# Attention block of a streaming encoder step: the stick leads, and cached memory keys are multiplied by masked queries that accumulate in place

## The chip, the cores and the metric

The kernel runs on one core of one Trainium2 chip. The metric is the device time of one execution in microseconds; of several runs the median is taken. Everything is float32.

## The reference, cut to what matters

One layer of an encoder is computed for a prompt of 1024 frames and for a batch of 8 samples of 16 frames each, which share the weights. The 8 x 16 sample frames are put together into one tile of 128 rows. After a combined projection there are three kinds of attention:

```
A (the "stick"): z = q.k/8; log_keep = -softplus(z) under a strict causal mask;
   weight = exp(log_sigmoid(z) + sum of log_keep of the later keys); out = weight @ v      8 heads of 64
B (the "window"): softmax over 128 past keys and the own chunk, with ALiBi and sinks       8 q heads, 2 kv heads of 64
M (the "memory"): softmax over 256 memory tokens, no mask                                  4 heads of 128
```

Every one of the 8 samples has its own caches: 128 past keys and values for A, 128 for B, 256 for M. A query of sample b may meet the cached keys of sample b alone. After the attention come the gated output projection and a retrieval of single experts (128 per frame) from a table of 16384, which takes most of the time and is not touched.

## The kernel before, in words

`build` (1600s) calls three blocks in turn, `project`, `attend` and `experts`. A block is a program per engine; the next one begins when all engines have come to its end.

`attend` works on tiles of 128 queries: 8 of the prompt (t = 0 to 7) and the sample tile (t = 8, called ST). Its order is written by the class `Course`. It deals out everything to ticks `tau`, and every engine walks through the ticks in order, doing at each whatever the course lists for it. Engines aren't tied to one tick together: only semaphores hold them.

- **Stick.** A step is one tile of queries against one tile of keys; each step occupies two ticks, each tile one more. Step k has its products with the keys at its first tick (`score`, PE, L756), then the chain Abs, Exp, Ln on ScalarE (L809 to L813), the softplus and its mask on VectorE (L837, L843), the sum over later keys as a product with a triangle (`suffix`, PE, L624 and L627), the weights (L770, or L852, L775 and L868 for the first step of a tile), and six ticks after the score the product with the values (L687). The order of tiles is 0, ST, 1, 2, ... 7, the first step at tick 4. The second step of ST is against the cached keys: 8 samples by 8 heads of small products, 64 rows by 128 keys, 16 queries each, from the tile `cache`, which `cache_kT` fills; later `cache` takes the cached values.
- **Window and memory.** 27 units (t, c), three per tile, ST first: c = 0 and 1 are halves of the window's heads, c = 2 is the memory attention. A unit makes its logits (`wscore`, PE, L642 to L650), adds a bias and takes the maximum on VectorE (L882, L888), exponentiates on ScalarE (L789), normalises (L910), is transposed on PE (L699) and copied (L797), and multiplied with the values. The units stand every three ticks from tick 7 on, and seven ticks after unit 2. The logits of all of them lie in PSUM banks 4 and 5.
- **Cached keys of window and memory** (`mul`, ticks 1 to 4, L653 to L667). For each sample b, 8 products for the memory (`kmem[b]`, 128 keys as the stationary operand, 16 query columns moving; L661) and 2 for the window (`kwcT`, 64 columns; L666). The results have keys in rows, so ScalarE copies them out of PSUM (`past_m` L800, `past_w` L801) and the units of ST transpose them back with the identity (L644, L650). `kmem` has three buffers, which SyncE refills as `mul_done` counts. The cached values of the memory go through the same buffers at ticks 19 to 22 (`past_values`, L738).

SyncE issues the loads in this order: bias, sinks, `kwcT`, `vwc`, `kmem` for samples 0 to 2, `cache_kT`. PSUM banks 0 to 3 hold the stick's logits, 4 and 5 the units' logits, 6 the transposes and outputs of the units, 7 the output of the stick. GpSimd does nothing in this block.

The heart of the old arrangement, in code:

```
for kk in range(2):
    for h in range(MH):
        nc.tensor.matmul(ps[:, 4 + kk, h * P + b * DS:h * P + (b + 1) * DS],
                         kmem[:, b % 3, h * MT + kk * P:h * MT + (kk + 1) * P], qm[:, h, c], start=True, stop=True)
```

Of the kernel before, what the change touches and what calls it, by code (L numbers as in the profile page):

```python
# [24 lines left out]
P = 128  # L25
# [3 lines left out]
ST = PT  # L29
# [408 lines left out]
class Course:  # L438


    def __init__(self):
        self.steps = []
        b = 4
        self.order = [0, ST] + list(range(1, ST))
# [17 lines left out]
        self.mul_at = 1  # L462
        self.win = []
        b = self.mul_at + 6
        for u in range(len(self.units)):
            self.win.append(b)
            b += 7 if u == 2 else 3
# [28 lines left out]
def attend(nc, A, S, wide_dram, o_d):  # L496
# [7 lines left out]
    with ExitStack() as ctx:  # L504
# [8 lines left out]
        vcache = cache[:, :].rearrange("p (b n) -> p b n", b=DB)  # L513
        bias = sb("bias", [P, SWH, 2 * P])
# [4 lines left out]
        past_m = sb("past_m", [P, 2, MH, P])  # L519
# [24 lines left out]
        kw_in = sem("kw_in")  # L544
        km_in = [sem(f"km_in{i}") for i in range(3)]
        mul_done = sem("mul_done")
        past_kept = sem("past_kept")
# [19 lines left out]
        def _(sp):  # L567
# [8 lines left out]

            sp.dma_start(bias[:, :, :].rearrange("p h k -> p (h k)"), wide_dram[:, BW:2 * BW]).then_inc(bias_in, 16)
            sp.dma_start(sink[:, :], A["sinks"][0:1, :].to_broadcast([P, SWH])).then_inc(sink_in, 16)
            sp.dma_start(kwcT[:, :, :].rearrange("p b s -> p (b s)"), A["cache_swa_kT"]).then_inc(kw_in, 16)
            sp.dma_start(vwc[:, :, :], A["cache_swa_v"][0].rearrange("b s h d -> s b (h d)")).then_inc(kw_in, 16)  # L580
            for n in range(3):
                load_mem(n)
            sp.dma_start(kcache, A["cache_kT"]).then_inc(kc_in, 16)
            for tau in range(C.length):
# [9 lines left out]
                if tau in C.mul:  # L594
                    k = C.mul[tau]
                    for b in range(2 * k, 2 * k + 2):
                        sp.wait_ge(mul_done, b + 1)
                        load_mem(b + 3)
                if tau in C.wfront and C.wfront[tau] == 2:
# [15 lines left out]

        @block.tensor
        def _(pe):
            for tau in range(C.length):
# [10 lines left out]
                if tau in C.wscore:  # L629
# [4 lines left out]
                    if t == ST and c == 0:  # L634
                        pe.wait_ge(past_kept, 2)
                    out = ps[:, 4:6, :].rearrange("p a (j k) -> p (a j) k", k=2 * P)
                    cols = slice(t * P, (t + 1) * P)
                    for i in (0, 2, 1, 3):
# [7 lines left out]
                        elif t < ST:  # L646
                            last = nc.tensor.matmul(out[:, i, :], qm[:, i, cols], mk[:, i, :], start=True, stop=True)
                        else:
                            for kk in range(2):
                                last = nc.tensor.transpose(out[:, i, kk * P:(kk + 1) * P], past_m[:, kk, i, :], ident)  # L650
                    last.then_inc(w_logits, 1)
                if tau in C.mul:
                    m = C.mul[tau]  # L653
                    if m == 0:
                        pe.wait_ge(kw_in, 32)
# [1038 lines left out]
```

## Time and profile before

| | us |
|---|---|
| median of 3 runs | 4359.3 (4357.4 to 4360.08) |
| the profiled execution, its own time | 4359.77 |
| span of that execution | 4357.9 |
| of it the block of attention, 429.6 to 903.3 us | 473.7 |
| TensorE busy, share of the span | 82% |
| VectorE / ScalarE / GpSimd busy | 60% / 34% / 40% |

The span is the stretch that the profile covers; the execution's own time is 1.9 us longer. Busy times of TensorE (PE) are sums over its matrix products, whose ends are modelled; PEld is the loading of stationary operands. PEclk in a row is the clock granted to TensorE as a share of its full speed: 0.50 is 1.2 GHz, 1.00 is 2.4 GHz. One float32 product of the program stands as two PE instructions in the trace, a transpose as one.

### The profile page before, as it was taken

To read this page: it belongs to the slowest core of one execution; us is meant where nothing else is said; L and a number is where in the kernel's file an instruction comes from. 1 tells how busy PE (TensorE), PEld (TensorE's weight loads), DVE (VectorE), ACT (ScalarE), POOL (GpSimd) and SP (SyncE) were. 2 spreads that over 40 slices of the span, in tenths; PEclk is the share of its full clock that TensorE was granted. 3 is DMA by queue.
4 is the path that set the end of the run, shared out by engine and by line. 5 is a ranking of instruction groups with operands and counts; after the bars stand their busy time and mean duration, and the time that the engine had idled before them with its cause. 6 is when DMAs were issued, how large, how long until landed. Compare 5 with 4: busy or idle time off the path is not lost.

```text
span 4357.9 us, 35532 instructions
## 1 busy us (share of the span) xinstructions
PE 3565.2 (82%) x11041; PEld 1831.4 (42%) x11041; DVE 2595.4 (60%) x5556; ACT 1491.4 (34%) x3932; POOL 1744.5 (40%) x1430
## 2 busy tenths in 40 slices
PE   7999888889668898858888888996777777778777
PEld 4545655568434445423333345442333333333222
DVE  2130256621778954866876876676676676676444
ACT  2111256721343334343333335344222222223222
POOL 0000000000456677666676666667333333333332
PEclk9999589999879999979998998998999999999999
DMA  5111310044889899999999999999999999999998
GB/s 168 56 38 59 113 42 20 16 145 167 335 330 387 350 420 422 407 385 421 421 421 421 411 419 421 421 397 417 421 421 421 419 420 417 414 416 412 422 421 355
DMA packets 246270, 1415.48 MB, mean 325 GB/s; under 512 B 26417, under 2 KB 58417, under 8 KB 92721
## 3 DMA queue, kind: packets, MB, share of 16 engines
q0 software_dynamic: 165888, 1208.03, 67.4%
q1 hardware_dynamic: 80192, 205.18, 12.7%
q8 instruction: 87, 1.43, 0.1%
q14 instruction: 103, 0.84, 0.1%
HBM read 1374.85 MB, written 39.19 MB: 324 GB/s over the span
## 4 chain that ended last, share of the span: by engine, by line
DMA 24%; POOL 17%; PE 15%; DVE 11%; issue 10%; ACT 3%; POOLq 0%; SPq 0%; ACTq 0%; DVEq 0%
DMA ring<-in_experts_dram,idx 24%; POOL side L1232 9%; PE ps L1342 8%; POOL ring L1221 7%; DVE ring L1596 4%; PE ps L1313 2%; PE ps L1265 2%; PE ps L1290 1%; ACT diag L1440 1%; DVE cand L1471 1%; PE ps L1275 1%; DVE hot L1486 1%; DVE hot L1482 1%; DVE idx L1490 1%; DVE part L1479 1%
## 5 line engine op out<-in xcount | busy, mean ns | idle before, releaser
L1342 PE MATMUL ps<-ring,diag 128*128 128x512 f32 x3520 | 1794.6, 655 | 655.7 <-ACT diag L1440 642.1
L1221 POOL DMA_INDIRECT ring<-in_experts_dram,idx x1152 | 1101.4, 956 | 2528.4 <-PE ps L1342 1281.0
L1596 DVE CUSTOM_DVE_ANT_0 ring<-ring,ps 128x1024 f32<-128x1024 f32 x1152 | 1385.8, 1220 | 877.7 <-DMA ring<-in_experts_dram,idx 864.5
L1342 PEld LDWEIGHTS ps<-ring,diag 128*128 128x128 f32 x3520 | 696.6, 206 | 1659.1 <-ACT diag L1440 909.8
L1424 ACT ACTIVATE act_<-hid 128x2 f32<-128x2 f32 x576 | 117.1, 203 | 2021.7 <-DVE hid L1596 2016.2
L1232 POOL TENSOR_TENSOR side<-side,ring 128x1024 f32<-128x1024 f32 x272 | 642.6, 2362 | 56.2 <-ACT ring L1445 50.7
L1265 PE MATMUL ps<-hx,wbuf 128*128 128x256 f32 (+2 forms) x1152 | 402.9, 494 | 13.6 <-DMA hx<-hT_scratch 13.0
L1440 ACT ACTIVATE diag<-const,wgt 128x128 f32<-128x128 f32 x880 | 320.5, 396 | 19.5 <-PE ps L1342 0.7
L1445 ACT ACTIVATE ring<-ring,wgt 128x1024 f32<-128x1024 f32 x272 | 308.1, 1133 | 0.0
L1265 PEld LDWEIGHTS ps<-hx,wbuf 128*128 128x128 f32 x1152 | 224.6, 195 | 184.0 <-issue 118.1
L309 PE MATMUL ps<-w_qkv,hT 128*128 128x512 f32 (+1 forms) x720 | 285.1, 552 | 1.3 <-DVE mhT L403 1.3
L1431 ACT ACTIVATE wgt<-act_,gw 128x1 f32<-128x1 f32 x1152 | 276.8, 287 | 19.8
L1313 PE MATMUL ps<-hx,wbuf 128*128 128x256 f32 (+2 forms) x768 | 269.8, 500 | 13.8 <-ACT mixn L1393 12.6
L837 DVE SCALAR_TENSOR_TENSOR sps<-ps,za 128x512 f32<-128x512 f32 x76 | 52.4, 690 | 277.3 <-ACT za L813 277.3
L1313 PEld LDWEIGHTS ps<-hx,wbuf 128*128 128x128 f32 x768 | 152.3, 199 | 131.8 <-issue 98.1
L1275 PE MATMUL ps<-o_x,wbuf 128*128 128x256 f32 (+2 forms) x576 | 203.5, 490 | 0.0
L309 PEld LDWEIGHTS ps<-w_qkv,hT 128*128 128x128 f32 x720 | 134.8, 191 | 132.0 <-issue 126.4
L412 DVE TENSOR_REDUCE nrm<-stage 128x4 f32<-128x512 f32 (+2 forms) x29 | 16.3, 562 | 239.4 <-ACT stage L355 239.4
L1275 PEld LDWEIGHTS ps<-o_x,wbuf 128*128 128x128 f32 x576 | 111.3, 193 | 84.2 <-issue 58.5
L1290 PE MATMUL ps<-wbuf,mixn 128*128 128x256 f32 x576 | 129.8, 382 | 1.6 <-DVE mixn L1540 1.6
L1290 PEld LDWEIGHTS ps<-wbuf,mixn 128*128 128x128 f32 x576 | 110.7, 192 | 29.3 <-issue 15.4
L624 PE MATMUL ps<-sps,const 128*128 128x512 f32 x152 | 93.6, 701 | 25.6 <-DVE sps L843 19.6
(174 smaller groups left out, 2782.8 us busy)
## 6 DMA issues: line engine op xcount, KB each, us to landing
wbuf<-in_w_gate_o_dram SPq DMA_DIRECT2D x72, 768.0 KB
wbuf<-in_w_q_dram SPq DMA_DIRECT2D x24, 1024.0 KB
ring<-in_experts_dram,idx POOLq DMA_INDIRECT x1152
wbuf<-in_w_out_dram SPq DMA_DIRECT2D x12, 1024.0 KB
w_qkv<-in_w_in_dram SPq DMA_DIRECT2D x5, 2048.0 KB, 8.2
o_x<-o_scratch SPq DMA_DIRECT2D x9, 768.0 KB, 26.6
s<-s_scratch SPq DMA_DIRECT2D x6, 1024.0 KB, 11.1
hT_scratch<-hT SPq DMA_DIRECT2D x9, 512.0 KB, 6.7
```

Of the source, the lines that this page charges most:

```text
L309: last = nc.tensor.matmul(ps[:, bank(u), 0:n], src[:, k, t * P:(t + 1) * P], w[:, c % 2, k, 0:n], start=(k == 0), stop=(k == KC - 1))
L1221: i = nc.gpsimd.indirect_dma_start(out=ring[:, j % RING, :], out_offset=None, in_=A["experts"], in_offset=bass.IndirectOffsetOnAxis(ap=idx ...
L1232: nc.gpsimd.tensor_tensor(side[:, m % 2], side[:, m % 2], ring[:, j % RING, DM:2 * DM], ALU.add).then_inc(side_done, 1)
L1265: last = nc.tensor.matmul(ps[:, 4 + u % 2, 0:N].rearrange("p (i t) -> p i t", t=P), w[:, k * P:(k + 1) * P], hx[:, 0:n, k, :], start=(k == ...
L1275: last = nc.tensor.matmul(ps[:, 6 + u % 2, 0:N].rearrange("p (i t) -> p i t", t=P), w[:, k * P:(k + 1) * P], o[:, 0:n, b, k - KC, :], star ...
L1290: last = nc.tensor.matmul(ps[:, 4 + x % 4, 0:2 * P], mixn[:, k * N + i * P:k * N + (i + 1) * P], w[:, k * 2 * P:(k + 1) * 2 * P], start=(k ...
L1313: last = nc.tensor.matmul(ps[:, 4 + x % 2, 0:N].rearrange("p (i t) -> p i t", t=P), w[:, c:c + P], hx[:, 0:n, k, :], start=(k == 0), stop= ...
L1342: last = nc.tensor.matmul(acc[:, h, :], diag[:, (by_pe(j) - 1) % 4, :], ring[:, j % RING, DM + h * HB:DM + (h + 1) * HB], start=(j % SLOTS ...
L1431: last = nc.scalar.activation(wgt[:, i:i + 1], act_[:, i:i + 1], ACT.Copy, scale=gw[:, m % 2, i:i + 1])
L1440: last = nc.scalar.activation(diag[:, d % 4, :], ident, ACT.Copy, scale=wgt[:, j % SLOTS:j % SLOTS + 1])
L1445: nc.scalar.activation(v, v, ACT.Copy, scale=wgt[:, j % SLOTS:j % SLOTS + 1]).then_inc(scaled, 1)
L1596: last = nc.vector.tensor_tensor_reduce(out=u, in0=u, in1=xp, scale=1.0, scalar=0.0, op0=ALU.mult, op1=ALU.add, accum_out=hid[:, j % SLOTS ...
```

## The change

- The stick begins at tick 0 and not 4, and the order of tiles is 0, 1, 2, 3, ST, 4 to 7. Its steps on ST are at ticks 24 and 26.
- The window's products with `kwcT` all go to tick 2, into PSUM banks 5 and 6; a single copy (`past_w`) follows. `kwcT` is the first load.
- The units of ST begin at ticks 4, 7 and 13; those of the prompt stay at ticks 20, 23, ... 89. The course is 97 ticks long as before.
- The products with the cached memory keys go to ticks 10 to 13, two samples each. GpSimd clears the tile `cache` and writes into it, for each sample and head, the queries of the sample tile with zeros in place of all other samples' queries (`qz`). That is the stationary operand now, 256 keys move, and the 8 samples accumulate on one another in PSUM banks 4 and 5. What stands there in the end are the logits of unit 2 with queries in rows: `past_m`, its copy and its transposes are gone.
- The stick's first values no longer wait for the two copies, and the window's values of unit 0 wait for `vwc` by a semaphore of its own.
- `cache_kT` is loaded into `cache` only when these products are done (SyncE, tick 14).

```diff
@@ class Course
-        b = 4
-        self.order = [0, ST] + list(range(1, ST))
+        b = 0
+        self.order = [0, 1, 2, 3, ST] + list(range(4, ST))
@@
-        self.mul_at = 1
-        self.win = []
-        b = self.mul_at + 6
-        for u in range(len(self.units)):
+        self.swa_at = 2
+        self.mul_at = 10
+        self.win = [4, 7, self.mul_at + 3]
+        b = self.win[2] + 7
+        for u in range(3, len(self.units)):
             self.win.append(b)
-            b += 7 if u == 2 else 3
+            b += 3
@@ attend
+        qz = cache[:, :].rearrange("p (h b q) -> p h b q", h=MH, b=DB)
-        past_m = sb("past_m", [P, 2, MH, P])
@@ sync
+            sp.dma_start(kwcT[:, :, :].rearrange("p b s -> p (b s)"), A["cache_swa_kT"]).then_inc(kw_in, 16)
             sp.dma_start(bias[:, :, :].rearrange("p h k -> p (h k)"), wide_dram[:, BW:2 * BW]).then_inc(bias_in, 16)
             sp.dma_start(sink[:, :], A["sinks"][0:1, :].to_broadcast([P, SWH])).then_inc(sink_in, 16)
-            sp.dma_start(kwcT[:, :, :].rearrange("p b s -> p (b s)"), A["cache_swa_kT"]).then_inc(kw_in, 16)
-            sp.dma_start(vwc[:, :, :], A["cache_swa_v"][0].rearrange("b s h d -> s b (h d)")).then_inc(kw_in, 16)
+            sp.dma_start(vwc[:, :, :], A["cache_swa_v"][0].rearrange("b s h d -> s b (h d)")).then_inc(vw_in, 16)
             for n in range(3):
                 load_mem(n)
-            sp.dma_start(kcache, A["cache_kT"]).then_inc(kc_in, 16)
@@
                     for b in range(2 * k, 2 * k + 2):
-                        sp.wait_ge(mul_done, b + 1)
+                        if b < DB - 1:
+                            sp.wait_ge(mul_done, b + 1)
+                        else:
+                            sp.wait_ge(w_logits, 3)
                         load_mem(b + 3)
+                if tau == C.mul_at + 4:
+                    sp.wait_ge(w_logits, 3)
+                    sp.dma_start(kcache, A["cache_kT"]).then_inc(kc_in, 16)
@@ new: GpSimd
+        @block.gpsimd
+        def _(pool):
+            nc.gpsimd.memset(cache[:, :], 0.0).then_inc(zeroed, 1)
+            pool.wait_ge(zeroed, 1)
+            for b in range(DB):
+                c = slice(b * DS, (b + 1) * DS)
+                last = nc.gpsimd.tensor_copy(qz[:, :, b, c], qm[:, :, ST * P + b * DS:ST * P + (b + 1) * DS])
+            last.then_inc(qz_done, 1)
@@ tensor
-                if tau in C.wscore:
+                if tau in C.wscore and C.wscore[tau] != 2:
@@
-                        pe.wait_ge(past_kept, 2)
+                        pe.wait_ge(past_kept, 1)
@@
+                if tau == C.swa_at:
+                    pe.wait_ge(kw_in, 16)
+                    for b in range(DB):
+                        c = slice(ST * P + b * DS, ST * P + (b + 1) * DS)
+                        for gg in range(KVH):
+                            r = slice(gg * HD, (gg + 1) * HD)
+                            out = ps[:, 5 + gg, :].rearrange("p (j q) -> p j q", j=GRP)[:, :, b * DS:(b + 1) * DS]
+                            last = nc.tensor.matmul(out, kwcT[r, b, :], qw[r, :, c], start=True, stop=True)
+                    last.then_inc(swa_done, 1)
                 if tau in C.mul:
                     m = C.mul[tau]
                     if m == 0:
-                        pe.wait_ge(kw_in, 32)
+                        pe.wait_ge(qz_done, 1)
+                        pe.wait_ge(w_exped, 2)
                     for b in range(2 * m, 2 * m + 2):
-                        c = slice(ST * P + b * DS, ST * P + (b + 1) * DS)
                         pe.wait_ge(km_in[b % 3], 16 * (b // 3 + 1))
...
-+                        for h in range(MH):
+                            last = nc.tensor.matmul(ps[:, 4 + h // 2, (h % 2) * MT:(h % 2 + 1) * MT], qz[:, h, b, :], kmem[:, b % 3, h * MT:(h + 1) * MT],
+                                                    start=(b == 0 and h % 2 == 0), stop=(b == DB - 1), skip_group_check=True)
+                        last.then_inc(mul_done if b < DB - 1 else w_logits, 1)
...
@@ scalar
-                if tau == C.mul_at + 4:
-                    act.wait_ge(mul_done, DB)
-                    nc.scalar.activation(past_m[:, :, :, :].rearrange("p k h q -> p (k h q)"), ps[:, 4:6, :].rearrange("p a n -> p (a n)"), ACT.Copy).then_inc(past_kept, 1)
-                    nc.scalar.activation(past_w[:, :, :].rearrange("p h q -> p (h q)"), ps[:, 6:8, :].rearrange("p a n -> p (a n)"), ACT.Copy).then_inc(past_kept, 1)
+                if tau == C.swa_at:
+                    act.wait_ge(swa_done, 1)
+                    nc.scalar.activation(past_w[:, :, :].rearrange("p h q -> p (h q)"), ps[:, 5:7, :].rearrange("p a n -> p (a n)"), ACT.Copy).then_inc(past_kept, 1)
```

## Rows read from the trace of the kernel before

**Rows 1.** The page: its span and the busy time of each engine

```profile
span 4357.9 us, 35532 instructions
...
PE 3565.2 (82%) x11041; PEld 1831.4 (42%) x11041; DVE 2595.4 (60%) x5556; ACT 1491.4 (34%) x3932; POOL 1744.5 (40%) x1430
```

**Rows 2.** Stretches of attention: length, busy time by engine, TensorE clock, DMA share, GB/s

```profile
429.60:473.90 44.30, 32.89 (x160) 31.79 (x160) 0.00 (x0) 1.28 (x1) 0.00 (x0) 0.52 0.61 214
473.90:518.70 44.80, 36.30 (x212) 26.39 (x210) 17.38 (x29) 16.47 (x32) 0.00 (x0) 0.50 0.17 59
518.70:554.00 35.30, 27.94 (x342) 19.54 (x340) 16.82 (x30) 20.89 (x47) 0.00 (x0) 0.94 0.16 46
554.00:592.60 38.60, 38.59 (x234) 28.20 (x234) 17.87 (x29) 13.20 (x29) 0.00 (x0) 0.78 0.32 89
592.60:876.50 283.90, 244.94 (x1805) 153.97 (x1804) 174.10 (x299) 198.28 (x456) 0.00 (x0) 0.98 0.06 17
876.50:903.30 26.80, 20.86 (x157) 14.65 (x156) 12.96 (x22) 12.45 (x32) 0.00 (x0) 0.94 0.11 30
```

**Rows 3.** Timeline, 441 to 474 us: start, duration, engine, operation, idle time before it

```profile
441.01 3.57 PE L661 MATMUL ps<-qmT,kmem 128*128 128x16 f32 x16 [12.21 <-DMA kmem<-in_cache_mem_kT_dram]
...
444.51 0.69 PE L666 MATMUL ps<-qswT,kwcT 64*128 64x64 f32 x4
...
473.92 1.83 PEld L756 LDWEIGHTS ps<-qsbT,ksbT 64*128 64x128 f32 x16
```

**Rows 4.** Transfer of the window's cached keys, issue to landing

```profile
DMA to landing us min/median/max: 7.4/7.4/7.4
```

**Rows 5.** Timeline of the stick's start, 474 to 492 us

```profile
474.02 2.02 PE L756 MATMUL ps<-qsbT,ksbT 64*128 64x128 f32 x16
...
477.92 1.01 ACT L800 ACTIVATE past_m<-ps 128x1024 f32<-128x1024 f32 x1
...
479.51 2.07 PE L624 MATMUL ps<-sps,const 128*128 128x512 f32 x2 [3.47 <-DVE sps L843]
...
483.15 2.08 PE L624 MATMUL ps<-sps,const 128*128 128x512 f32 x2 [1.56 <-DVE sps L843]
...
489.13 2.12 PE L756 MATMUL ps<-qsbT,ksbT 64*128 64x128 f32 x15
```

**Rows 6.** Timeline: cached keys and values of the stick, and a product at the clock's rise

```profile
499.73 10.83 PE L756 MATMUL ps<-qsbT,cache 64*128 64x16 f32 x100
...
518.71 1.66 PE L624 MATMUL ps<-sps,const 128*128 128x512 f32 x2
...
537.88 3.91 PE L687 MATMUL ps<-wts,cache 128*64 128x16 f32 x128
```

**Rows 7.** Timeline: cached memory values (128x16), memory logits of a prompt tile (128x256)

```profile
565.94 3.74 PE L738 MATMUL ps<-PTs,kmem 128*128 128x16 f32 x32
...
887.19 1.89 PE L647 MATMUL ps<-mkT,qmT 128*128 128x256 f32 x8
```

**Rows 8.** Waits from 592.6 to 876.5 us: us in total, times, longest

```profile
DVE sps L837 <- ACT za L813: 96.6, 44, 4.6
...
ACT za L809 <- PE ps L756: 31.0, 21, 3.9
```

**Rows 9.** GpSimd's instructions, grouped by line

```profile
L1232 POOL TENSOR_TENSOR side<-side,ring 128x1024 f32<-128x1024 f32 x272 | 642.6, 2362 | 56.2 <-ACT ring L1445 50.7
...
L260 POOL MEMSET kswT<- 128x128 f32 x1 | 0.2, 206 | 0.3 <-POOLq L1659 0.3
```

**Rows 10.** Short stretches about an idle time of TensorE, columns as in group 2

```profile
530.00:533.00 3.00, 0.99 (x2) 0.16 (x2) 2.93 (x5) 0.17 (x1) 0.00 (x0) 1.00 0.00 0
533.00:536.00 3.00, 2.24 (x14) 1.94 (x16) 2.24 (x5) 0.60 (x1) 0.00 (x0) 0.58 0.00 0
536.00:540.00 4.00, 4.00 (x83) 3.02 (x82) 0.93 (x2) 3.03 (x7) 0.00 (x0) 0.89 0.02 4
```

**Rows 11.** Timeline: the first product of the next block

```profile
915.49 5.53 PE L1265 MATMUL ps<-hx,wbuf 128*128 128x256 f32 x16 [13.00 <-DMA hx<-hT_scratch]
```

More of the change, by code:

```diff
@@ L544, in attend @@
         kw_in = sem("kw_in")
+        vw_in = sem("vw_in")
         km_in = [sem(f"km_in{i}") for i in range(3)]
         mul_done = sem("mul_done")
+        swa_done = sem("swa_done")
+        zeroed = sem("zeroed")
+        qz_done = sem("qz_done")
         past_kept = sem("past_kept")
@@ L645, in _ @@
                             last = nc.tensor.matmul(out[:, i, P:2 * P], qw[r, j, cols], kw[r, NT * P:(NT + 1) * P], start=True, stop=True)
-                        elif t < ST:
+                        else:
                             last = nc.tensor.matmul(out[:, i, :], qm[:, i, cols], mk[:, i, :], start=True, stop=True)
-                        else:
-                            for kk in range(2):
-                                last = nc.tensor.transpose(out[:, i, kk * P:(kk + 1) * P], past_m[:, kk, i, :], ident)
                     last.then_inc(w_logits, 1)
+                if tau == C.swa_at:
[7 more added lines that the diff above has]
+                    last.then_inc(swa_done, 1)
                 if tau in C.mul:
@@ L654, in _ @@
                     if m == 0:
-                        pe.wait_ge(kw_in, 32)
+                        pe.wait_ge(qz_done, 1)
+                        pe.wait_ge(w_exped, 2)
                     for b in range(2 * m, 2 * m + 2):
-                        c = slice(ST * P + b * DS, ST * P + (b + 1) * DS)
                         pe.wait_ge(km_in[b % 3], 16 * (b // 3 + 1))
-                        for kk in range(2):
-                            for h in range(MH):
-                                nc.tensor.matmul(ps[:, 4 + kk, h * P + b * DS:h * P + (b + 1) * DS],
-                                                 kmem[:, b % 3, h * MT + kk * P:h * MT + (kk + 1) * P], qm[:, h, c], start=True, stop=True)
-                        for gg in range(KVH):
-                            r = slice(gg * HD, (gg + 1) * HD)
-                            out = ps[:, 6 + gg, :].rearrange("p (j q) -> p j q", j=GRP)[:, :, b * DS:(b + 1) * DS]
-                            last = nc.tensor.matmul(out, kwcT[r, b, :], qw[r, :, c], start=True, stop=True)
-                        last.then_inc(mul_done, 1)
+                        for h in range(MH):
+                            last = nc.tensor.matmul(ps[:, 4 + h // 2, (h % 2) * MT:(h % 2 + 1) * MT], qz[:, h, b, :], kmem[:, b % 3, h * MT:(h + 1) * MT],
+                                                    start=(b == 0 and h % 2 == 0), stop=(b == DB - 1), skip_group_check=True)
+                        last.then_inc(mul_done if b < DB - 1 else w_logits, 1)
                 if tau in C.values:
@@ L674, in _ @@
                             pe.wait_ge(st_kept, C.nth(t))
-                        else:
-                            pe.wait_ge(past_kept, 2)
                     else:
@@ L704, in _ @@
                     pe.wait_ge(pt_kept, 2 * u + 2)
+                    if u == 0:
+                        pe.wait_ge(vw_in, 16)
                     probs = lambda i, kk: PTs[:, (2 * i + kk) * P:(2 * i + kk + 1) * P]
```

## The prediction

> **What bounds the kernel now.** I read the page first: TensorE is busy for 82% of the span, more than any other engine, but that is a mean over three blocks [rows 1]. The change lies in attention alone, so the table by stretches comes next [rows 2]. Attention runs from 429.6 to 903.3 us, and the next block cannot start before all engines have left it: its first product is at 915.49 us after 13.00 us without PE work, which end with a transfer that is issued only then [rows 11]. So what attention gains or loses at its end shifts all that follows by the same amount, and I forecast that end.
>
> The stretches show three regimes. From 429.6 to 473.9 us nothing but the cached-key products runs: VectorE does nothing, ScalarE one table load, and PE waits for `kmem` at first (12.21 us, part of which lies before the block) [rows 2, 3]. In the timeline the stick's first product comes right behind, at 473.92 us. The clock is 0.50 throughout. From 473.9 to 518.7 us it is still 0.50, and from then on mostly full. In the steady stretch from 592.6 to 876.5 us PE is busy for 244.94 of 283.90 us and ScalarE for 198.28; the waits there are VectorE on ScalarE's chain and that chain on the stick's logits [rows 8]. PE is thus close to the bound, and its order within a tick feeds the chain.
>
> As a yardstick, that stretch goes from the score of tick 24 to that of tick 86, 62 ticks: 4.58 us a tick. Ticks 11 to 18 took 35.30 us, 4.41 a tick. The clock matters for narrow products as well: 16 of them (128x16) took 3.57 us at 0.50, 32 took 3.74 us near 1.00, so 0.223 against 0.117 us each [rows 3, 7]. Had they run at full clock, the 128 old memory products would have taken 15 us and not 28.6.
>
> **The change part by part, as a timetable of attention.** The removed front is 473.9 - 430.0 = 43.9 us: after it the stick's first product starts at 430.0.
>
> *Ticks 0 to 3.* The old start, score at 474.02, suffixes at 479.51 and 483.15, next score ending at 491.25, took 17.2 us at 0.50; it held 3.9 us of unit 0's logits between 485.2 and 489.1 [rows 5]. The new one has no logits of a unit there, but the 16 window products of `kwcT`. Four of their instructions take 0.69 us at 0.50 [rows 3], about 0.62 net of overlap, so 8 samples take 5.0 us. The copy of `past_m` (1.01 us, which stood ahead of the chain's second half) is gone, that of `past_w` is behind both halves. The first suffix can start at 5.5 us, so PE is then busy without a gap: 435.5 + 2.1 + 5.0 + 2.1 + 2.1 = 447. `kwcT` landed 7.4 us after its issue with a megabyte ahead of it [rows 4]; it is now first, so at 437 at the latest, when PE wants it at 437.6. Its new wait has the second suffix and score 1 queued behind it and through them the whole chain; I cost it at nothing (0 to 2 us).
>
> *Ticks 4 to 9.* These are 6 ticks of ordinary work: 26.4 us at 4.41. At half clock PE's own work is the bound: logits of units 0 and 1 (2 x 3.9), suffixes (2.1 three times, 4 twice with `later`), two scores, two values, two transposes: 31 us. I take 28, with the clock rising within. Tick 10 starts at 475.
>
> *Ticks 10 to 13.* To each, two samples are added: 8 samples by 4 heads are 32 products, 64 instructions with 256 columns moving. Eight such took 1.89 us at full clock, 1.73 net of the last one's overlap [rows 7]: 64 are 14 us. At 0.50 they would be 28. They stand ahead of the score, so they delay the chain and are not hidden beside it; only PE's idle share (14%, some 2 us) takes a part. Four ticks are 18.3 + 14 - 2 = 30, and tick 14 starts at 505. The clock is what separates 14 from 28. The rows of the steady stretch show 0.98 with PE idle 14% of the time, and one loss: after 3 us with 0.99 busy the next stretch had 0.58 and the one after 0.89 [rows 2, 10]. These new products are wide and leave no gaps, so I take the full clock. The Trainium skill speaks against it: in "TensorE: Matmul & The Clock Gate", section "Loop structure matters more than you think", products that stand between waits run at the low clock; by it this term is 28 us and attention ends 14 us later (the rival of half clock below).
>
> *What they wait for.* `qz_done`: GpSimd clears 4096 elements a row and makes 8 copies of 64. By its clearing of 128 elements in 206 ns that is at most 6.6 us, by its two-input addition (1024 in 2362 ns) 9.4 us [rows 9]; the copies add 1 to 2. It ends by 442, 33 us early; cover gone only if GpSimd is five times slower. `kmem` for samples 0 to 2 arrives as before, at 441 or sooner. Later samples have over 7 us a tick to come. SyncE now waits for the stick's output of tile 1 ahead of the load for sample 7: 0 to 2 us, taken as 0. `cache_kT`, once `cache` is free at tick 14, has 12 ticks until it is wanted. The eight transposes of `past_m` (1 us) vanish.
>
> *Ticks 14 to 18.* 5 x 4.41 = 22: to 527. *Ticks 19 to 23* have the same work as before, cached memory values included, which with its clock of 0.78 took 38.6 us [rows 2]: to 566.
>
> *Ticks 24 to 81.* 58 x 4.58 = 265.6. In them now lie the stick's cached keys, 128 narrow instructions. They took 13.8 us at 0.50 (100 in 10.83 us [rows 6]); scaled as above they are 7.3 at full clock. Less the ordinary score, that adds 6 to 12.6; they leave PE's array mostly idle, and the clock may fall behind them, so I take 10. The cached values took 3.91 against 1.1 us: 2.8 more. That leads to 844. In the Trainium skill, same page, section "LDWEIGHTS (loading the stationary operand)", a load of 128 columns takes 107 ns at either clock; by that the keys always cost 13.7 us and the end comes some 2.6 us later. Rows 3 and 7 show that the load-bound product follows the clock.
>
> *Tick 82 to the end.* The stick's last score was at tick 86 and is at tick 82, while the units stay at their ticks. Before, 26.8 us were left after it [rows 2]. Now four more ticks lie between it and the last unit. With one unit at a time each engine waits for the other, about 7 us for three ticks (logits 1.5, VectorE 3, ScalarE 2.5), so 9 us more; at least 5, at most 4 x 4.58 = 18. 844 + 26.8 + 9 = 880.
>
> **Sum.** Attention ends at 880 and not at 903.3: 23 us earlier. Against the profiled execution's span of 4357.9 this is 4335, with 1.9 us around it 4337. That execution's own time, 4359.77, lies 0.5 above the median of the runs shown, so the median comes to 4336. A difference of 0.2%, 9 us, is about what a measurement of this kernel can tell from none.
>
> **The rivals.**
>
> *Half clock in ticks 4 to 13.* The chain's start leaves PE with gaps, as between 474 and 496. For it: 0.50 until 518.7 before. Against it: those gaps came from work that was too little per tick, and the rise at 518.7 (two wide products in 1.66 us where 2.07 was the price [rows 5, 6]) came after 8 us of dense ordinary products, which the new ticks 2 to 7 offer too. It costs 14 us at the cached keys and 5 in the ticks: attention ends near 899, time 4355, no change. Chance 0.10.
>
> *The gain is larger.* The end is less ragged and the cached keys go by at full clock (-6 together), the new products fill the slack of the chain (-4): 4325. What speaks for it: 96.6 us of waits of VectorE for the chain [rows 8]. Chance 0.15.
>
> *Slower.* The clock stays low from the start through the stick's cached keys at tick 26. A steady tick has 3.95 us of PE work at full clock, near 7 at half, so each loses about 2.3 us. It needs 14 us at the memory keys and 8 more ticks at half clock to eat the 23 us; if 22 such ticks in 4 to 31 are slow, the loss is 14 + 50 - 23: 4400. Before, ticks 11 to 18 had 0.94 under the same load, which speaks against it. Chance 0.03.
>
> *It doesn't do what it says.* A late tile, `kwcT` or a `kmem` buffer, takes the place of the old wait: 12 us at most, as before, and the end is at 892, time 4348. Chance 0.09.
>
> **How the numbers follow.** The forecast has a chance of 0.63, within 4330 to 4345 for its terms (start 0 to 4, tail -4 to +9, cached keys -4 to +3). With the larger gain below and the late tile above, the range is 4322 to 4350; half clock and slower lie outside. Faster by over 0.2% is under 4350.6: 0.63 + 0.15 + 0.09, and a little of half clock, 0.88. Within 0.2%: 0.09. Slower: 0.03.
>
> **What the changed profile would show.** Right: the first stick product at 430, nothing idle at the block's head; the window products ahead of the second suffix; 64 instructions 128x256 on `kmem` in all 14 us at a clock near 1.00; the attention's end near 880; a last unit after the stick with PE half idle. Wrong: 0.50 in the row of ticks 10 to 13, PE's wait on `kwcT`, `kmem` or GpSimd, more than 13 us at the stick's cached keys, or over 40 us from the last stick score to the end. If the end moves and the whole does not by the same amount, the claim that attention's end gates the next block is false.

## The result and the profile after

The changed kernel takes 4312.94 us (median of 5 executions, 4311.97 to 4328.63) beside 4357.54 for the kernel before (5 executions), a ratio of 0.9911 with a 95% interval of 0.99 to 0.9921. I had forecast 4336, 4322 to 4350: the direction was right and the gain nearly twice as large, outside the range. Two more series, of the same code, gave 4318.19 and 4327.40. The 15 executions of all three have a median of 4319.1; they lie between 4312.0 and 4319.1 or between 4326.1 and 4330.9, with none between.

The page of the profiled execution, which took 4311.97 us:

```profile
span 4310.2 us, 35396 instructions
...
PE 3524.2 (82%) x10969; PEld 1800.8 (42%) x10969; DVE 2591.9 (60%) x5556; ACT 1490.8 (35%) x3931; POOL 1746.8 (41%) x1439
```

Stretches of attention, cut at the ticks that the prediction used (PE begins a tick with its suffix, and 24 and 82 are cut at their score, as in the prediction): 0 to 3, 4 to 9, 10 to 13, 14 to 18, 19 to 23, 24 to 81, and the rest; columns as in [rows 2].

```profile
427.10:441.60 14.50, 10.87 (x69) 7.36 (x69) 4.20 (x6) 6.42 (x9) 5.45 (x9) 0.67 0.72 255
441.60:464.30 22.70, 18.61 (x108) 10.96 (x108) 17.39 (x30) 15.80 (x36) 0.00 (x0) 0.91 0.05 13
464.30:491.10 26.80, 26.79 (x212) 20.61 (x212) 11.10 (x19) 13.57 (x26) 0.00 (x0) 1.00 0.50 146
491.10:509.60 18.50, 14.84 (x105) 8.91 (x101) 7.34 (x12) 9.48 (x21) 0.00 (x0) 0.82 0.52 201
509.60:542.00 32.40, 32.40 (x238) 24.21 (x238) 16.36 (x27) 15.34 (x32) 0.00 (x0) 1.00 0.37 106
542.00:816.30 274.30, 240.79 (x1893) 158.02 (x1892) 164.14 (x281) 183.71 (x422) 0.00 (x0) 0.95 0.08 25
816.30:856.40 40.10, 28.36 (x213) 20.11 (x212) 18.60 (x32) 17.75 (x52) 0.00 (x0) 0.91 0.07 20
```

Attention now goes from 427.1 to 856.4 us, 429.3 in place of 473.7, 44.4 less. The project block before it happened to end 2.5 us earlier. What follows did not change: from its first product to the end of the span are 3441.6 us, and were 3442.4 [rows 1, 11]. So the claim that the end of attention gates the rest holds. The most telling columns are PE busy and PEclk: PE's work in ticks 19 to 23 has become shorter at the same count of ordinary steps, with the clock at 1.00 where [rows 2] had 0.78. Added up over stretches of 4 us, weighed by their clock, TensorE stood at 0.50 for some 126 us of attention before and 55 now. Of these 55, some 14 lie at the stick's cached keys and right behind them (551 to 571 us). Some 21 more begin at two idle times of PE: 14 at the start of the block, behind 3.56 us, and 7 at tick 17, behind 3.66 us; both stand in the timeline that follows.

Steps of the timetable in the timeline of the changed kernel, PE alone:

```profile
427.17 1.16 PE L776 MATMUL ps<-qsbT,ksbT 64*128 64x128 f32 x16 [0.83 <-PEq L87]
...
431.89 2.07 PE L643 MATMUL ps<-sps,const 128*128 128x512 f32 x2 [3.56 <-DVE sps L862]
433.90 3.68 PE L675 MATMUL ps<-qswT,kwcT 64*128 64x64 f32 x32
...
437.50 2.07 PE L643 MATMUL ps<-sps,const 128*128 128x512 f32 x2
...
465.28 3.66 PE L685 MATMUL ps<-kmem,cache 128*128 128x256 f32 x16
...
501.83 2.07 PE L643 MATMUL ps<-sps,const 128*128 128x512 f32 x2 [3.66 <-DVE sps L862]
...
552.02 11.34 PE L776 MATMUL ps<-qsbT,cache 64*128 64x16 f32 x128
...
563.28 2.07 PE L643 MATMUL ps<-sps,const 128*128 128x512 f32 x2
...
868.61 3.77 PE L1284 MATMUL ps<-hx,wbuf 128*128 128x256 f32 x8 [13.01 <-DMA hx<-hT_scratch]
```

A pair of suffix instructions (L643) is a good gauge of the clock: it takes about 1.1 us at 1.00 and 2.07 at 0.50. The first score starts at once, the window's products stand ahead of the second suffix, and the masked products of two samples (16 instructions) take 3.66 us at full clock. The stick's cached keys take 11.34 us at tick 26, begun at full and ended at half clock, and the suffix behind them still costs 2.07 us.

GpSimd's part, grouped by line:

```profile
L628 POOL MEMSET cache<- 128x4096 f32 x1 | 3.5, 3516 | 426.0 <-POOLq L87 426.0
L632 POOL COPY cache<-qmT 128x64 f32<-128x64 f32 x8 | 1.9, 290 | 0.1
```

### The profile page after: what moved, and what is told of

Same layout as the page of the kernel before. It is cut to its first block, busy times and chain, and to the rows that moved or that the text cites. A ratio compares the mean times of both kernels' runs of the same rounds, so it can differ in the third digit from the quotient of the medians.

```text
span 4310.2 us, 35396 instructions
## 1 busy us (share of the span) xinstructions
PE 3524.2 (82%) x10969; PEld 1800.8 (42%) x10969; DVE 2591.9 (60%) x5556; ACT 1490.8 (35%) x3931; POOL 1746.8 (41%) x1439
## 4 chain that ended last, share of the span: by engine, by line
DMA 24%; POOL 17%; PE 15%; DVE 12%; issue 10%; ACT 3%; POOLq 0%; SPq 0%; ACTq 0%; DVEq 0%
DMA ring<-in_experts_dram,idx 23%; POOL side L1251 10%; PE ps L1361 8%; POOL ring L1240 8%; DVE ring L1615 4%; PE ps L1332 2%; PE ps L1284 2%; PE ps L1309 1%; PE ps L1294 1%; ACT diag L1459 1%; DVE cand L1490 1%; DVE hot L1505 1%; DVE hot L1501 1%; DVE part L1498 1%; DVE idx L1509 1%
```

## The experiments

Times are medians in us, with the ratio to the kernel before, run in the same series, and its 95% interval. The experiments ran in four series, and the kernel before had 4359.6 to 4361.5 us in them; where two runs of different series are compared, the ratios are the fairer measure. "Attention" is read from the one profiled execution, from the block's first instruction to the copy of the last unit's output.

| kernel | time | ratio | attention |
|---|---|---|---|
| before | 4357.5 to 4361.5 | 1 | 473.6 |
| stick first alone | 4358.5 | 0.9997 (0.9988 to 1.0007) | 471.0 |
| stick first, sample tile late | 4349.5 | 0.9981 (0.9971 to 0.9991) | 467.0 |
| the same, masked wide products at ticks 1 to 4 | 4331.2 | 0.9935 (0.9919 to 0.9952) | 449.8 |
| changed kernel, three series | 4312.9, 4318.2, 4327.4 | 0.9911, 0.9906, 0.9922 | 429.2, 430.2, 440.0 |
| changed, narrow products at ticks 10 to 13 | 4338.8 | 0.9945 (0.9927 to 0.9964) | 457.1 |
| the same, 128 columns each | 4320.9 | 0.9907 (0.9893 to 0.992) | 442.8 |
| before, masked products alone | 4347.0 | 0.9967 (0.9958 to 0.9977) | 464.7 |
| masked products and stick first, old order | 4358.9 | 1.0002 (0.9993 to 1.0011) | 474.6 |
| changed, masked stick keys | 4322.7 | 0.9915 (0.9902 to 0.9929) | 435.8 |
| changed, values split | 4314.6 | 0.9898 (0.9882 to 0.9915) | 429.9 |
| both of these | 4313.7 | 0.9902 (0.9887 to 0.9918) | 429.2 |

**Stick first alone.** The old course with one number changed:

```diff
-        b = 4
+        b = 0
```

> The kernel before with the stick's steps beginning at tick 0 and nothing else changed: cached memory keys in the old narrow form at ticks 1 to 4, tile ST second. The first score runs at once, but the second score stands behind samples 0 to 5 of the cached keys, which still wait for the transfer (441 us) and run at 1.20 GHz (4.15 us a sample). Theory 'clock': narrow products keep the clock low whatever stands between them, so only the start-up of the first step (about 15 us of idle PE between 474 and 489) is hidden: 10 to 16 us faster, 4342 to 4348. Rival 'order': most of the 44 us comes from the stick leading, so 25 us or more faster, under 4333.

Neither theory had it: no gain. PE in its timeline:

```profile
429.47 1.16 PE L756 MATMUL ps<-qsbT,ksbT 64*128 64x128 f32 x16 [0.83 <-PEq L87]
...
440.83 3.57 PE L661 MATMUL ps<-qmT,kmem 128*128 128x16 f32 x16 [10.20 <-DMA kmem<-in_cache_mem_kT_dram]
...
468.96 2.02 PE L756 MATMUL ps<-qsbT,ksbT 64*128 64x128 f32 x16
```

The first score runs at 429.47, but PE works in order, the second stands behind six samples, and these wait for the transfer as before; it comes at 468.96. That is 5 us earlier than the old first score at 474.0. The units of the window now end further behind the stick: 41.1 us from its last score to the end, 26.8 before [rows 2], and of the cached keys' cost nothing is saved, 13.84 us at half clock.

**The order of tiles in addition.**

```diff
-        self.order = [0, ST] + list(range(1, ST))
+        self.order = [0, 1, 2, 3, ST] + list(range(4, ST))
```

> The run in which the stick's steps begin at tick 0 and all else is old, with the new order of tiles in addition (0, 1, 2, 3, sample, 4 to 7). The stick's cached keys then no longer follow directly on the narrow products of ticks 1 to 4. Theory 'clock': between the two narrow blocks the clock has risen, so the cached keys take 11 and not 13.9 us, and the ticks behind the front are ordinary and fast: 5 to 12 us faster than the run with the old order, 4347 to 4354. Rival 'order is nothing': within 3 us of it, 4356 to 4361.

9 us faster than the run before it (7 by the ratios, as the series differ), within the range of theory "clock". Its cached keys took 8.8 us where they had taken 13.8.

**The masks in addition, still at ticks 1 to 4** (the products as in the change; their result is copied once, and unit 2 reads the copy).

> Stick from tick 0, new order of tiles, masked wide products, but these still at ticks 1 to 4, where PE waits for the first transfer until 439 us with the stick's second score behind. The run with the old order of tiles lost its gain to a wait for the stick's keys (8 us) and the narrow keys at half clock behind it; both are gone here. Theory 'clock': masked against narrow products is worth 10 to 16 us beside the run with the late sample tile alone, and what is still missing to the changed kernel is the waiting at the front (10 us) and a little more: 4326 to 4336. Rival 'place is nothing': equal to the changed kernel, 4313 to 4320.

18 us faster again in the same series, a little more than the 10 to 16 that theory "clock" expects, and 12 from the changed kernel's 4319 over all its executions. The stretch from the first sample's product to the last one's, columns as in [rows 2], with the narrow products of the run before:

```profile
440.70:479.10 38.40, 38.37 (x180) 34.98 (x180) 4.75 (x7) 4.75 (x8) 0.00 (x0) 0.50 0.49 166
```

and with the masked ones:

```profile
440.40:463.40 23.00, 22.93 (x117) 16.82 (x117) 3.63 (x6) 4.75 (x8) 0.00 (x0) 0.91 0.53 172
```

The same eight samples, two suffixes and one score stand in both, and PE is busy without a gap in both. 38 us at 0.50 have become 23 at 0.91, though both begin at 0.50 behind the same wait of 10 us. The two differ in more than the width, as the masked form also has half as many instructions.

**Narrow products at the new place.** The changed kernel with the old form at ticks 10 to 13 (with its copy and its transposes, and unit 2 one tick later):

```diff
-                        for h in range(MH):
-                            last = nc.tensor.matmul(ps[:, 4 + h // 2, (h % 2) * MT:(h % 2 + 1) * MT], qz[:, h, b, :], kmem[:, b % 3, h * MT:(h + 1) * MT],
...
+                        for kk in range(2):
+                            for h in range(MH):
+                                last = nc.tensor.matmul(ps[:, 4 + kk, h * P + b * DS:h * P + (b + 1) * DS],
+                                                        kmem[:, b % 3, h * MT + kk * P:h * MT + (kk + 1) * P], qm[:, h, c], start=True, stop=True)
```

> The changed kernel with the old narrow products for the cached memory keys (16 columns moving, 128 instructions, copy and transposes back), at the same ticks 10 to 13, unit 2 one tick later. At equal clock both forms cost PE 14 to 15 us, so theory 'order' (the masked queries are worth nothing but the copy and the transposes) gives 2 to 4 us more than the changed kernel. Theory 'clock': the narrow products drop TensorE to half clock there and it stays low into the ticks behind, as at 558 to 564 and 573 to 588 us before; then it is 10 to 20 us slower than the changed kernel and the stretch of these products shows 0.5 to 0.8.

The four groups of these products in PE's timeline:

```profile
469.35 6.25 PE L690 MATMUL ps<-qmT,kmem 128*128 128x16 f32 x32
...
482.11 6.85 PE L690 MATMUL ps<-qmT,kmem 128*128 128x16 f32 x32
...
494.55 4.26 PE L690 MATMUL ps<-qmT,kmem 128*128 128x16 f32 x32
...
504.74 4.22 PE L690 MATMUL ps<-qmT,kmem 128*128 128x16 f32 x32
```

The stretch that holds them, columns as in [rows 2]:

```profile
469.30:509.00 39.70, 39.70 (x237) 34.04 (x238) 10.41 (x18) 11.02 (x20) 0.00 (x0) 0.60 0.32 94
```

20 us slower than the changed kernel, and 0.60 is the clock of the stretch, in which PE is never idle. **Then the decisive one**: the same instructions with the same stationary operands, copy and transposes, but the moving operand eight times as wide:

```diff
-                                last = nc.tensor.matmul(ps[:, 4 + kk, h * P + b * DS:h * P + (b + 1) * DS],
-                                                        kmem[:, b % 3, h * MT + kk * P:h * MT + (kk + 1) * P], qm[:, h, c], start=True, stop=True)
+                                last = nc.tensor.matmul(ps[:, 4 + kk, h * P:(h + 1) * P],
+                                                        kmem[:, b % 3, h * MT + kk * P:h * MT + (kk + 1) * P], qz[:, h, b, :],
+                                                        start=(b == 0 and h == 0), stop=(b == DB - 1), skip_group_check=True)
```

> The run with the old narrow products at ticks 10 to 13 (keys stationary, copy and transposes back), but every product moves 128 columns in place of 16: the masked queries of all samples, accumulated. The same 128 instructions with the same stationary operands, eight times the columns, the same transposes and copy. If what TensorE moves decides its clock (theory 'clock'), the four groups of these products last 3.8 us each in place of 6.25, 6.85, 4.26 and 4.22 us, the clock is near 1.00 there and attention comes to 430 to 437 us, 4313 to 4322 in all, though more is computed. If the gain of the changed kernel over the narrow form comes from fewer instructions, fewer waits or the missing copy and transposes (rival 'work'), it stays at 457 us of attention and 4330 to 4342.

The same groups in PE's timeline:

```profile
468.18 5.41 PE L690 MATMUL ps<-cache,kmem 128*128 128x128 f32 x32
...
477.06 3.73 PE L690 MATMUL ps<-cache,kmem 128*128 128x128 f32 x32
...
483.96 3.74 PE L690 MATMUL ps<-cache,kmem 128*128 128x128 f32 x32
...
490.97 3.73 PE L690 MATMUL ps<-cache,kmem 128*128 128x128 f32 x32
```

And their stretch:

```profile
468.00:508.00 40.00, 37.55 (x341) 30.07 (x340) 14.31 (x24) 19.80 (x40) 0.00 (x0) 0.93 0.56 189
```

More is computed and it is 18 us faster (17 by the ratios), and no execution of the one is as fast as the slowest of the other (4326.5 to 4344.4 against 4313.0 to 4325.3). 14 us of it lie in the attention of the profiled executions; three of the four groups take 3.7 us, the first 5.41 (I had expected 3.8 for each). The transposes and the copy remain, and nothing is seen of them: 4320.9 against the changed kernel's 4319.1. Its attention, 442.8, is above the 437 I had allowed; this profile shows the clock down again between 521 and 556 us, at the cached memory values (see the spread, below).

**Masks alone, and masks with stick first in the old order.**

> The kernel before with only the masked queries: the products of the cached memory keys in the new wide form, still alone at ticks 1 to 4 ahead of the stick; the result is copied out once, and unit 2 reads that copy without transposes. The transfers still land at 441 us. Theory 'clock': the wide products lift the clock within some 5 us, so the front falls from 33 to 20 us, and the stick's start and its cached keys begin at full clock instead of 0.50: 13 us in the front plus 5 to 10 behind it, 4335 to 4341. Rival 'order': the form matters only in the front's own length at the old half clock (64 x 0.43 = 28 us against 28.7), so within 3 us of the kernel before.

15 us (4347.0, the kernel before at 4361.5 in that series), less than the 20 to 26 expected, and the rival falls. The front gave what was expected of it, 20.5 us in place of 33. What did not come is the gain behind it. PE in its timeline:

```profile
462.81 1.11 PE L766 MATMUL ps<-qsbT,ksbT 64*128 64x128 f32 x16
...
467.39 2.07 PE L637 MATMUL ps<-sps,const 128*128 128x512 f32 x2 [3.47 <-DVE sps L855]
...
484.60 13.84 PE L766 MATMUL ps<-qsbT,cache 64*128 64x16 f32 x128
```

The first score still runs at full clock. Then PE waits 3.47 us for the stick's chain, comes back at 0.50, and stays there until some 507 us, with more such waits and the narrow cached keys on the way. So narrow products are not the only thing that takes the clock: the start of the stick's chain does it too, where nothing stands between its first score and its first suffix.

> The kernel before with both halves of the idea but not the place: stick from tick 0, and masked wide products still at ticks 1 to 4 ahead of the second score. PE still waits for the first transfer until 441 us with the second score behind it. Theory 'clock' with 'place': only one of the two gains adds up, because 10 us of waiting stay and the stick's second score comes at 462 us or so (14 us of products, 5 of the window's, 4 of suffixes after 441): attention 455 to 463 us, 4337 to 4345. Rival: place doesn't matter once stick and mask are in, 430 to 435 us, 4313 to 4320.

A miss: 4358.9, no gain at all where theory "clock" had 4337 to 4345. The queries share the tile `cache` with the stick's keys, whose load has to wait for them, and with the sample tile second they are wanted at once. PE in its timeline:

```profile
470.93 13.84 PE L766 MATMUL ps<-qsbT,cache 64*128 64x16 f32 x128 [8.05 <-DMA cache<-in_cache_kT_dram]
484.70 2.07 PE L637 MATMUL ps<-sps,const 128*128 128x512 f32 x2
```

PE had waited 8.05 us for that load, and where it had been at full clock before (a suffix in 1.13 us at 461.75), the cached keys now ran at 0.50. With the sample tile late, the shared buffer costs nothing.

**The spread of the executions.**

The changed kernel again, unedited, twice.

> The changed kernel once more. Attention took 429.7 us where the forecast had 450, and TensorE stood at half clock for some 55 us of it where the kernel before had 127. Five executions of it were two near 4327 and three near 4312 us. Theory 'clock': the 15 us between the two are the clock falling at other places in attention or behind it; a profile of an execution near 4327 would show more stretches at 0.50. Rival 'transfers': the 15 us lie in the experts block, whose gathers fill the DMA engines, and attention lasts 430 us in both. Both expect 4312 to 4329.

The executions took 4312.64 to 4330.51, but the profiled execution was a short one (4315.98), attention 430.2.

> The changed kernel a third time, for the spread of its executions beside the next run. By theory 'narrow runs' some of the executions again lie near 4328, the others near 4314; four executions of the kernel with the split values lay within 3 us. If all of these lie within 6 us too, the spread was not a property of this code.

Here the profiled execution took 4329.37 us. PE at ticks 19 to 22, in the first profile of the changed kernel and, in the second fence, in this one:

```profile
511.39 3.64 PE L758 MATMUL ps<-PTs,kmem 128*128 128x16 f32 x32
...
519.03 3.74 PE L758 MATMUL ps<-PTs,kmem 128*128 128x16 f32 x32
...
525.54 3.75 PE L758 MATMUL ps<-PTs,kmem 128*128 128x16 f32 x32
```

The longer execution:

```profile
513.75 4.19 PE L758 MATMUL ps<-PTs,kmem 128*128 128x16 f32 x32
...
519.88 2.07 PE L643 MATMUL ps<-sps,const 128*128 128x512 f32 x2
...
524.63 4.98 PE L758 MATMUL ps<-PTs,kmem 128*128 128x16 f32 x32
...
534.42 4.57 PE L758 MATMUL ps<-PTs,kmem 128*128 128x16 f32 x32
...
544.24 3.98 PE L758 MATMUL ps<-PTs,kmem 128*128 128x16 f32 x32
```

With the same instructions, attention took 440.0 us and not 429.2, and the stick's score of tick 24 came 126.5 us after the block's start where it had come after 114.8. The narrow products of the cached memory values lost the clock in one execution and kept it in the other, and their neighbours took 2.07 in place of 1.1 us. Of the 17.4 us between the two, 10.8 are in attention, 4.4 in the experts block (3446.0 against 3441.6) and 2.1 in the project block. The profiles of all kernels show 3433.5 to 3446.0 us for the experts; why was not tried, and it stays open. So theory "clock" has most of the difference and not all of it, as rival "transfers" has its 4 us.

**The values split.** Of the two samples of a tick one stands behind the suffix, the other behind the score.

```diff
+                if tau in C.past_values:
+                    m = C.past_values[tau]
...
+                    for b in (2 * m,):
...
                 if tau in C.wscore and C.wscore[tau] != 2:
...
                     last.then_inc(z_done, 1)
+                if tau in C.past_values:
+                    m = C.past_values[tau]
+                    for b in (2 * m + 1,):
```

> The changed kernel with the cached memory values of ticks 19 to 22, narrow products still, taken apart: of the two samples of a tick the first stands right behind the suffix and the second behind the score, so that 16 narrow instructions stand together in place of 32, with the same work. Profiles of the changed kernel had 1.00 there and 32.4 us for these five ticks, the run with masked stick keys 0.78 and about 39 with the same code ahead of that place. Theory 'narrow runs': long runs of narrow products are where executions of one kernel part into 4312 and 4328; with short runs the clock stays at 1.00 each time, the five executions lie within 6 us, at 4311 to 4317. Rival: what counts is the share of narrow work in these ticks, however it is dealt out; then the executions spread as before, 4312 to 4330.

Four executions within 3 us (4312.99 to 4315.87). Only at tick 22 is there nothing to stand between the two samples, and there the clock falls. PE's timeline of this run, ticks 21 and 22:

```profile
527.20 1.85 PE L656 MATMUL ps<-PTs,kmem 128*128 128x16 f32 x16
531.10 1.96 PE L785 MATMUL ps<-PTs,kmem 128*128 128x16 f32 x16
...
534.70 1.85 PE L656 MATMUL ps<-PTs,kmem 128*128 128x16 f32 x16
536.41 2.46 PE L785 MATMUL ps<-PTs,kmem 128*128 128x16 f32 x16
538.71 2.05 PE L643 MATMUL ps<-sps,const 128*128 128x512 f32 x2
```

Tick 21 has 1.85 us and, behind the score, 1.96; tick 22 then 1.85 and 2.46 for two samples together, and 2.05 for the suffix. Ahead of these ticks the profile has the same durations as the longer execution of the changed kernel (1.12, 0.94, 2.08 and 1.49 us from the suffix of tick 17 on): there the clock fell in tick 19, here it stayed at 1.00 up to tick 22. Against the rival speaks that the share of narrow work is the same. It rests on four executions and on this profile, and the last run below weakens what it says of the spread.

**The stick's keys by the same means.** GpSimd writes masked stick queries into the buffers of the memory values (now four) once these are done:

```diff
+            pool.wait_ge(w_pv, 3)
+            nc.gpsimd.memset(kmem[:, :, :], 0.0).then_inc(zeroed, 1)
...
+                last = nc.gpsimd.tensor_copy(qs[:, :, b, c], qT[:, :, ST * P + b * DS:ST * P + (b + 1) * DS])
```

> The changed kernel, and in addition the stick's own cached keys (ticks 26) by the same means: GpSimd clears the buffers of the cached memory values when they are done and writes the masked stick queries there, and each product moves 128 columns and accumulates. Theory 'clock': the 128 instructions take 8.7 us (16 ordinary ones take 1.16, 1.09 net) in place of 11.3, the clock stays at 1.00 behind them where it was 0.62 for 7 us, and the whole is 4 to 8 us faster than the changed kernel: 4305 to 4310. Rival 'port': GpSimd's clearing (3.5 us) and copies beside VectorE's work hold up VectorE by as much or come late and PE waits for them; then within 2 us of the changed kernel or slower.

PE at the keys, in its timeline:

```profile
562.12 7.42 PE L787 MATMUL ps<-kmem,cache 64*128 64x128 f32 x128
```

The keys take 7.4 us, not 11.3 (in other profiles without masks they took 8.8 to 9.1), and the next score comes 20.7 us after theirs, not 23.9. But from the score of the cached keys to the end of attention only 1.4 us are left of it (302.9 against 304.3), and this profile had lost the clock at the values before, in unchanged code. The whole, 4322.7, is over 12 us above the forecast range and within the rival's. The mechanism of rival "port" isn't seen all the same: GpSimd is done at 550.0 us, 12 us before the keys, and VectorE's product beside its clearing takes 1.23 us as elsewhere. Together with the split:

> The split cached memory values and the masked stick keys together. The masked keys alone took 7.3 us in place of 11.3 and shortened the way from one score to the next by 3.2 us, but that profile had lost the clock at the values before. With both, theory 'clock' expects 2 to 4 us less attention than 430, 4309 to 4313 in all, and executions within 6 us. Rival: GpSimd's clearing beside VectorE, or the clock lost elsewhere, takes it back: 4313 to 4325.

The four executions took 4308.91, 4313.54, 4313.92 and 4322.88 us. The lowest time of all runs is among them, but they lie 14 us apart where 6 had been forecast, so the split values do not make the executions agree. At tick 22, where 32 narrow instructions still stand together, this profile too lost the clock. In the same series the changed kernel had a median of 4327.4, and both kernels with the split are below its 4319 over all series, though the intervals of the ratios overlap; 4313.7 against 4314.6 doesn't tell whether the masked stick keys add anything.

## Why the prediction was wrong

- **The frame was right.** The end of attention gates the rest; the front's removal, the lack of waits for `kwcT`, `kmem` and GpSimd, the full clock of the new products and their price (14.5 us against 14) held. So did the price of the stick's cached keys, 11.3 us, 10.2 above an ordinary score, where the forecast took 10. None of the rivals for a smaller gain came: no half clock there, no late tile. One sign of being wrong did, just: 40.1 us from the last stick score to the end, over the 40 that were named.
- **The step that failed is the pace given to the ordinary ticks**, by terms: ticks 0 to 3 took 14.5 (17 forecast), 4 to 9 22.7 (28), 10 to 13 26.8 (30), 14 to 18 18.5 (22), 19 to 23 32.4 (38.6), 24 to 81 274.3 (278.4), the tail 40.1 (36). That is 20.7 us too much, the whole miss in attention. It has two parts.
- **Ticks 4 to 18, 12 us: a yardstick that held other work.** The 4.41 us a tick came from ticks 11 to 18 of the kernel before, and the 4.58 taken for ticks 10 to 13 from the steady stretch, where PE has 3.95 us of work a tick. Ticks 11 to 18 held the stick's cached values, 3.9 us against 1.1 [rows 6], which the forecast charges a second time in ticks 24 to 81, and the transposes of `past_m`, which it had itself counted as gone. PE's work was 3.49 us a tick there and 0.92 us it was idle [rows 2]. In the new ticks 4 to 9 it is 3.10 and 0.68, in 14 to 18 2.97 and 0.73, and in 10 to 13 3.1 without the new products, with no idle time. The clock is not the reason here: it was 0.94 in the yardstick and 0.91 and 0.82 in ticks 4 to 9 and 14 to 18. This part is read from rows; no run takes it apart. The forecast for ticks 4 to 9 was raised to 28 for a low clock besides, and that share is a matter of the clock.
- **Ticks 19 to 23, 6.2 us: the clock.** Here I wrote "the same work as before". The work was the same and the clock was not: the 38.6 us held a clock of 0.78, the 32.4 one of 1.00, PE never idle in either. That this run kept it is in part luck: the third series had a profile that lost it in these ticks. By the median of all 15 executions, 4319.1, the forecast of 4336 is 17 us too high, by the first series 23.
- **What the experiments add is where the gain of 44 us comes from.** I had priced the form of the products as equal at equal clock, 15 against 14 us. That is right and misses the point: in the runs the form goes with the clock, of these products and of their neighbours. It is worth 15 us alone at the front, 18 at the front with a late tile, 20 at ticks 10 to 13, and nothing with the stick first in the old order, where a load is waited for. Widened products with nothing else changed bring 17 to 18 of those 20. The new place, with what comes with it (`kwcT` first, the units of ST earlier, no wait of 10 us at the front), is worth 11 to 12, the order of tiles 9, stick first alone 1. Along the way from the kernel before to the changed one these are 1 + 9 + 18 + 12 us; by the ratios of each series they are 1 + 7 + 20 + 10.
- **The rule on loads** from the Trainium skill ("TensorE: Matmul & The Clock Gate", "LDWEIGHTS (loading the stationary operand)") gives one duration whatever the clock, 107 ns for 128 columns. The trace agrees at 0.50, where the 128 cached keys took 13.84 us, 108 ns each. It does not at full clock: the masked ones took 7.42 us, 58 ns each.
- **The rule on loops** from the same page of the Trainium skill ("Loop structure matters more than you think") speaks of long DMA waits between products, and the forecast read it as any wait. Ticks 10 to 13 had no idle time and ran at 1.00; ticks 4 to 9, with idle times of 2.0 us at most, ran at 0.91. So it did not bind there. Elsewhere idle times did cost the clock: PE came back at 0.50 from 3.56 and 3.66 us of it in the changed kernel, and from 3.47 in the one with masks alone. The other thing that went with a low clock, narrow products in a row with PE never idle, the forecast had in none of its cases but the stick's cached keys.
- The rival with the larger gain (4325) named the tail, the cached keys and the slack of the chain as its sources. The tail went the other way and the cached keys took what was forecast, so its direction was right for other reasons.

## What to carry to other kernels

When a narrow product is priced, look at the clock of its stretch and of the stretches behind it, and don't carry a duration from a throttled stretch to a changed neighbourhood. Zero-padding a 16-column moving operand to 128 columns, or swapping operands so that the wide one moves, cost TensorE nothing here and won 15 to 20 us, except where a wait for a load took the clock all the same. Where that isn't possible, breaking a run of narrow products up with wide ones is worth a try; it kept the clock for three ticks in both profiles that had it. A mean per tick is a price only for ticks with the same work: list what the ticks of the yardstick hold before it is carried over. Bringing work forward on one engine brings next to nothing (1 to 3 us here) while the next step stands, in that engine's order, behind work that waits for a transfer.

## What the runs showed of the hardware

- Eight times the moving columns took no more time: 32 instructions of 128x128 in 3.73 us against 3.74 for 32 of 128x16 at full clock [rows 7].
- PE was busy without a gap for 38 us of mostly narrow products and stayed at 0.50 throughout; with masked wide products in the same place it was at 0.50 for 3.8 us and at 1.00 for the 19 that followed.
- The clock fell to 0.50 with PE busy all the time, when 32 narrow instructions stood together (ticks 19 to 22), and one and the same program kept or lost it there from one execution to the next, which is 11 us of attention.
- GpSimd cleared 4096 elements a row in 3.5 us, half of what scaling its 128-element clearing gave (6.6).
- `kwcT` landed 3.5 us after its issue as the first load, 7.4 as the third [rows 4].
